# The rows of an expert block placed by a turned table of ranks

## The chip, the cores and the metric

The kernel runs on one core of a Trainium2 chip. The metric is the time of one execution on the device in microseconds (us); the median of several runs stands for the kernel. A core has TensorE (matmuls into PSUM), VectorE, ScalarE, GpSimd and SyncE (SP, which issues most transfers), and 16 DMA engines that carry all transfers between HBM and the on-chip memory (SBUF).

## The reference, cut to what matters

One inference step of one layer: a mixer (gated short convolution and sliding-window attention), a mixture of experts, and a gated per-layer embedding. 512 prompt tokens and 32 sample tokens pass through the same weights. The change touches only the mixture of experts:

```
logits = x @ w_router + b_router            # 544 tokens, 32 experts
top_v, top_i = top_k(logits, 4);  gate = softmax(top_v)
# for each expert e, on the tokens that chose it:
h = x @ w_up[e] + b_up[e]                   # 1024 -> 2048, glu and linear parts interleaved
act = min(glu, 7) * sigmoid(1.702 * min(glu, 7)) * (clip(lin, -7, 7) + 1)
y = act @ w_down[e] + b_down[e]             # 1024 -> 1024
out[token] = sum over its 4 experts of gate * y
```

All of it is in float32. 544 tokens with 4 experts each are 2176 pairs, 68 for an expert on average. In which order the tokens of one expert are computed doesn't matter to the result.

## The kernel before

After the mixer, the tokens' normalised rows (4 KB each) are written to a table m_rows in HBM. The router gives each token four experts. For each (token, expert) pair the kernel computes its rank among the tokens of that expert by matmuls with a triangular matrix (`rk0`), splits it into a lap (which block of the expert) and a `slot` below CAP = 96, and builds three things from it. The first two blocks have a short way of their own (`hot0`, `hot1`, lines 1511 and 1516), so that their gathers can start early. For all other blocks `slot_hots` (line 1591) makes a one-hot table `rank1` of slot against position: position p of a block is 1 where the table `iota` at p equals the pair's slot. Matmuls with it (`slot_rows`, line 2285) give, per block and position, the row number in m_rows (`rowi`), the row of the result table y_rows (`dsti`) and the gate (`gcol`). A position that no pair has gets a number beyond the table's end; the transfer of such a row is left out by its bounds check. `iota` holds 0, 1, 2, ..., so real rows are at positions 0 to n - 1 of a block with n tokens, and the padding is behind them.

The experts' loop runs over blocks of 96 positions (CAP = 32 * SETS); with these inputs there are 32, one for each expert. For block i:

- GpSimd gathers the rows: `rows_from` (line 692) is an indirect DMA from m_rows into `xg`, partition = position. VectorE transposes xg into xT (line 1650).
- TensorE multiplies: three bias matmuls (line 2259), then eight up chunks (line 2262) of 1 MB of w_up each; ScalarE and VectorE form the activation; VectorE transposes it (line 1659); four down chunks (line 2272) of 1 MB of w_down follow. The down matmuls of block i - 1 are done behind the up matmuls of block i.
- ScalarE and VectorE scale the result by the gate into `yrow` (lines 1014, 1639), and GpSimd scatters it to y_rows (`rows_to`, line 703), also an indirect DMA.

SP issues the weights (line 610). There are twelve chunk buffers `raw`, one block's worth: chunk l of the next block is issued when TensorE has used up chunk l of this one. Block STASH = 20 finds its first three chunks in three spare buffers (`ahead`) that were filled before the loop; one gate chunk for the layer's end (`gate_r`, line 620) is issued behind block 21.

The last block isn't scattered. Its result goes to the tokens by a matmul with `Sel` (line 1707), a one-hot table of token number (from `iota`) against the block's row numbers. At the end SP issues the last block's down chunks (line 632), three gate chunks (lines 634, 636, 638), and, once every scatter has landed, the rows of h and y_rows for each of five token tiles (lines 643 to 645). VectorE adds them (line 1731; for tiles 1 to 4 GpSimd sums pairs first, line 748); the embedding gate and the last norm follow. ScalarE rounds the gate chunks (line 1051) and VectorE splits them (line 1698).

`iota` is loaded by SP at line 556, between the last token tile's wait and its stores (lines 563 to 572), on the semaphore io_in, which line 1018 (ScalarE) and line 1508 (VectorE) wait for.

Of the kernel before, what the change touches and what calls it, by code (L numbers as in the profile page):

```python
# [13 lines left out]
F32 = mybir.dt.float32  # L14
# [7 lines left out]
P = 128  # L22
# [6 lines left out]
NT = 5  # L29
# [12 lines left out]
NEXP, TOPK = 32, 4  # L42
# [15 lines left out]
CAP = 32 * SETS  # L58
# [30 lines left out]
def build(nc, A, O):  # L89

    with ExitStack() as ctx:
        def sem(name):
            return ctx.enter_context(nc.semaphore(name))
# [5 lines left out]
        def at(name, shape, dt, off):  # L99
            n = int(np.prod(shape[1:])) * 4  # L100
            assert off + n <= 212800, (name, off + n)
            return nc.alloc_sbuf_tensor_at(name, shape, dt, offset=SB0 + off)
# [8 lines left out]
        R2 = R1 + 2 * KT * T * 4  # L111
# [89 lines left out]
        iota = at("iota", [P, P], F32, R2 + 4352)  # L201
        rank1 = at("rank1", [P, NT * TOPK, P], F32, R0)
# [3 lines left out]
        which = at("which", [P, NB], F32, R2 + 7168)  # L206
        plain = at("plain", [P, NB], F32, R2 + 7424)
        dstf = at("dstf", [P, NB], F32, R2 + 7680)
        bup = at("bup", [8, 512], F32R, R2 + 5120)
        bsel = at("bsel", [8, SETS, P], F32R, R2 + 35328)  # L210
        bself = at("bself", [8, SETS * P], F32, R1 + 16384)
        hot0 = at("hot0", [P, NT, P], F32, R2 + 7168)
        ent0 = at("ent0", [P, NT], F32, R2 + 9728)
        pad0 = at("pad0", [P, 1], F32, R2 + 9760)
        hot1 = at("hot1", [P, NT, P], F32, R2 + 9792)
# [180 lines left out]
        io_in = sem("io_in")  # L396
# [72 lines left out]
        def _(sp):  # L469
# [79 lines left out]
            for i in range(NT):  # L549
                if i == 1:  # L550
                    sp.wait_ge(tr_done, NT + 1)
                    sp.dma_start(raw[2][:], w_up[0, 2]).then_inc(landed[2], 16)
                if i == NT - 1:

                    sp.wait_ge(tiles_done, TB)
                    sp.dma_start(iota[:], A["c_iota"]).then_inc(io_in, 16)
                    sp.dma_start(bself[:], A["c_bsel"]).then_inc(io_in, 16)
                    for m in (4, 5):
                        sp.dma_start(raw[m][:], w_up[0, m]).then_inc(landed[m], 16)
                rows = slice(P * i, P * i + ROWS[i])  # L560
                sp.wait_ge(wo_ev, i + 1)
                if i < NT - 1:
                    sp.dma_start(h_dram[rows], hrow[:, i, :]).then_inc(h_out, 16)
                else:
                    for j in range(4):
                        sp.dma_start(h_dram[rows, QD * j:QD * j + QD], hrow[TS * j:TS * j + TS, i, 0:QD]).then_inc(h_out, 16)
                sp.wait_ge(m_done, i + 1)
                if i < NT - 1:
                    sp.dma_start(m_dram[rows], mrow[:, i % 2, :]).then_inc(rows_out[i % 2], 16)
                else:  # L570
                    for j in range(4):
                        sp.dma_start(m_dram[rows, QD * j:QD * j + QD], mrow[TS * j:TS * j + TS, i % 2, 0:QD]).then_inc(rows_out[0], 16)
# [179 lines left out]
        def _(act):  # L752
# [262 lines left out]
                                     scale=gcol[0:CAP, bass.ds(b, 1)]).then_inc(y_done, 1)  # L1015

            pp_copy(1)
            act.wait_ge(io_in, 32)
            nc.scalar.activation(bsel[:].rearrange("r b m -> r (b m)"), bself[:], ACT.Copy).then_inc(b_rnd, 1)
            pp_copy(2)  # L1020
            pp_copy(3)
# [142 lines left out]
        def _(dve):  # L1164
# [326 lines left out]
            for i in range(NT):  # L1491
# [10 lines left out]
                if i == 1:  # L1502
# [2 lines left out]
            b = R0S + ROUT * NT  # L1505

            nc.vector.tensor_tensor(ent0[:], mask[:, :, 0], tok1[:].rearrange("p (i k) -> p i k", k=TOPK)[:, :, 0], ALU.mult)
            dve.wait_ge(io_in, 32)
            dve.wait_ge(rk_mm, 1)
            place = ps[:, 0, 0:NT * NEXP].rearrange("p (i e) -> p i e", e=NEXP)  # L1510
            nc.vector.tensor_tensor(hot0[:], iota[:].unsqueeze(1).broadcast_to([P, NT, P]),
                                    place[:, :, 0].unsqueeze(2).broadcast_to([P, NT, P]), ALU.is_equal).then_inc(hot_done, 1)

            nc.vector.tensor_tensor(over[:], ps[:, 0, 200:201].broadcast_to([P, 2]), code[:, 1:3], ALU.is_gt).then_inc(r_step, 1)
            nc.vector.tensor_tensor(ent1[:], mask[:, :, 1], tok1[:].rearrange("p (i k) -> p i k", k=TOPK)[:, :, 0], ALU.mult)
            nc.vector.tensor_tensor(hot1[:], iota[:].unsqueeze(1).broadcast_to([P, NT, P]),
                                    place[:, :, 1].unsqueeze(2).broadcast_to([P, NT, P]), ALU.is_equal).then_inc(hot_done, 1)
            dve.wait_ge(r_step, b + 1)
            nc.vector.tensor_tensor(kov[:], over[:], code[:, 3:5], ALU.mult).then_inc(r_step, 1)
# [67 lines left out]
            def slot_hots(tiles):  # L1587

                for i in tiles:
                    mine = slice(TOPK * i, TOPK * i + TOPK)  # L1590
                    nc.vector.tensor_tensor(rank1[:, mine, :], iota[:].unsqueeze(1).broadcast_to([P, TOPK, P]),
                                            slot[:, mine].unsqueeze(2).broadcast_to([P, TOPK, P]), ALU.is_equal).then_inc(rank_hot, 1)

            def slot_table():
# [921 lines left out]
def constants():  # L2516
# [23 lines left out]
    for b in range(SETS):  # L2540
        bsel[[b, 4 + b], b, 0:CAP] = 1
        bsel[[SETS, 4 + SETS], b, CAP:] = 1
    out = {
        "c_fold": np.tile(np.eye(TS), (4, 1)),
        "c_ident": np.eye(P), "c_negd": negd, "c_biass": bias, "c_tok": tok, "c_code": code,
        "c_tri": p < np.arange(P)[None, :], "c_ones": np.ones((P, P)),
        "c_pad": TOPK * KROWS + 1 + p, "c_zero": np.zeros((T, D)), "c_bsel": bsel.reshape(8, SETS * P),
        "c_io16": np.broadcast_to(np.arange(MAXOVER), (P, MAXOVER)), "c_io32": np.broadcast_to(np.arange(NEXP), (P, NEXP)),
        "c_iota": np.broadcast_to(np.arange(P), (P, P)),
    }  # L2550
    return {k: np.ascontiguousarray(v.astype(f)) for k, v in out.items()}
```

## Time and profile before

| | |
|---|---|
| median of 3 runs | 1536.05 us (1535.56 to 1536.28) |
| the profiled execution | 1538.34 us, of which the span is 1536.50 us |
| TensorE busy | 1496.2 us, 97% of the span |
| VectorE, ScalarE, GpSimd busy | 48%, 16%, 7% |
| bytes moved | 492.04 MB, 320 GB/s over the span |
| the chain that ended last | TensorE 76%, DMA 10%, VectorE 5%, SP's queue 4% |

A block of the expert loop begins with its bias matmuls, so these mark the blocks in the trace: the first at 403 us, the last at 1395 us. Before them lie the mixer and the router, behind them the last sums and norms. The time to landing of a transfer counts from its issue on the queue until all of its parts, on all engines, have signalled. A chain of waits goes back from the last instruction to whatever released each step.

### The profile page before, as it was taken

Reading aid. Unit: us, or ns where it says so; the run is one execution under the profiler, and the core shown is the slowest. Engines: PE = TensorE matmul, PEld = TensorE weight load, DVE = VectorE, ACT = ScalarE, POOL = GpSimd, SP = SyncE. Lnnn points to the kernel's source line nnn. Section 1 sums busy time; section 2 is a strip of 40 time slices with the busy share of each in tenths; the row PEclk is TensorE's granted clock in tenths of the full one; section 3 lists DMA queues with packets and bytes.
Section 4 is the critical chain, followed back from the end, with each engine's and each line's share of the span. In section 5 each row is a group of like instructions: output and inputs, shape, how many; then the busy total and the mean of one; then the engine's idle time right before and its main releaser. Section 6 shows DMA issues by size and latency. Waiting matters only on the chain.

```text
span 1536.5 us, 38278 instructions
## 1 busy us (share of the span) xinstructions
PE 1496.2 (97%) x16304; PEld 854.4 (56%) x16304; DVE 731.9 (48%) x1619; ACT 243.2 (16%) x443; POOL 103.1 (7%) x136
## 2 busy tenths in 40 slices
PE   8999999999999999999999999999999999999697
PEld 7999999998543334433344333443334433334396
DVE  5457333353545434554345543455434554336584
ACT  5433323232200000000000000000000000001244
POOL 1000000000000000000000000000000000000050
PEclk9999999999999999999999999999999999999899
DMA  7411922352999999999999999999999999999841
GB/s 262 157 56 55 306 93 83 114 212 106 374 407 403 408 407 410 407 398 404 408 410 407 400 402 407 402 388 398 407 411 400 404 396 402 401 404 383 315 159 46
DMA packets 83474, 492.04 MB, mean 320 GB/s; under 512 B 13950, under 2 KB 19174, under 8 KB 30052
## 3 DMA queue, kind: packets, MB, share of 16 engines
q1 hardware_dynamic: 76260, 473.51, 78.4%
q0 software_dynamic: 7056, 17.56, 3.3%
q8 instruction: 49, 0.80, 0.2%
q14 instruction: 13, 0.11, 0.0%
q10 hardware_dynamic: 96, 0.07, 0.0%
HBM read 478.45 MB, written 29.79 MB: 331 GB/s over the span
## 4 chain that ended last, share of the span: by engine, by line
PE 76%; DMA 10%; DVE 5%; SPq 4%; ACT 2%; issue 1%; POOL 0%; DVEq 0%; ACTq 0%
PE ps L2262 36%; PE ps L2272 18%; PE ps L1913 9%; DMA raw<-w_up 6%; PE ps L2103 3%; SPq L610 2%; DMA raw<-w_ple_chunks 2%; PE ps L1853 1%; PE ps L2259 1%; PE ps L1854 1%; PE ps L1855 1%; DVE hq L1731 1%; PE ps L1977 1%; ACT S L836 1%; SPq L598 1%
## 5 line engine op out<-in xcount | busy, mean ns | idle before, releaser
L2262 PE MATMUL ps<-raw,xT 128*32 128x512 f32 x6072 | 660.7, 593 | 2.9 <-DMA raw<-w_up 2.7
L2262 PEld LDWEIGHTS ps<-raw,xT 128*32 128x32 f32 x6072 | 192.2, 110 | 454.4 <-issue 423.7
L2272 PE MATMUL ps<-raw,acT 128*32 128x256 f32 x6144 | 338.1, 379 | 3.1 <-DMA raw<-w_down_rows 3.1
L2272 PEld LDWEIGHTS ps<-raw,acT 128*32 128x32 f32 x6144 | 199.4, 110 | 149.0 <-issue 18.3
L1626 DVE TENSOR_SCALAR gl<-ps 128x256 f32<-128x256 f32 x96 | 34.8, 418 | 451.0 <-ACT gl L1009 451.0
L1659 DVE STREAM_TRANSPOSE acT<-arow 32x192 f32<-32x192 f32 x512 | 189.3, 370 | 7.4
L1650 DVE STREAM_TRANSPOSE xT<-xg 32x256 f32<-32x256 f32 x372 | 161.9, 435 | 13.8 <-DMA xg<-m_rows,ius 8.2
L1009 ACT ACTIVATE gl<-ps 128x256 f32<-128x256 f32 x96 | 29.9, 384 | 662.3 <-PE ps L2262 662.3
L1913 PE MATMUL ps<-aTh,wh 128*128 128x272 f32 x512 | 107.3, 291 | 1.5 <-DVE qTl L1317 1.0
L1913 PE MATMUL ps<-aTh,wl 128*128 128x272 f32 x512 | 106.0, 288 | 0.0
L1913 PE MATMUL ps<-aTl,wh 128*128 128x272 f32 x512 | 105.6, 288 | 0.0
L1168 DVE TENSOR_TENSOR wl<-raw,wh 128x2048 fp32r<-128x2048 f32 x21 | 48.1, 2290 | 80.4 <-ACT wh L756 80.4
L1913 PEld LDWEIGHTS ps<-aTh,wh 128*128 128x128 f32 x512 | 80.2, 188 | 2.8 <-DVE wl L1168 1.3
L1639 DVE TENSOR_SCALAR yrow<-ps,gside 32x256 f32<-32x256 f32 x93 | 45.6, 490 | 75.3 <-PE ps L2272 74.4
L1913 PEld LDWEIGHTS ps<-aTl,wh 128*128 128x128 f32 x512 | 80.5, 188 | 0.0
L1913 PEld LDWEIGHTS ps<-aTh,wl 128*128 128x128 f32 x512 | 80.0, 189 | 0.0
L1014 ACT ACTIVATE yrow<-ps,gcol 96x768 f32<-96x768 f32 x31 | 27.8, 897 | 294.6 <-PE ps L2272 294.6
L692 POOL DMA_INDIRECT xg<-m_rows,iug x29 | 28.7, 991 | 387.7 <-DVE iug L1531 361.2
L697 POOL COPY iug<-rowi 128x1 uint32 x28 | 9.3, 331 | 574.0 <-DVE xT L1650 574.0
L756 ACT ACTIVATE wh<-raw 128x2048 fp32r<-128x2048 f32 x21 | 40.1, 1911 | 20.7 <-PE ps L1913 11.4
L703 POOL DMA_INDIRECT y_rows<-yrow,ius x30 | 28.4, 947 | 160.2 <-issue 160.2
L1853 PE MATMUL ps<-gate_h,nTh 128*128 128x256 f32 x128 | 38.2, 299 | 0.2 <-DVE nTl L1783 0.2
(385 smaller groups left out, 1310.3 us busy)
## 6 DMA issues: line engine op xcount, KB each, us to landing
raw<-w_up SPq DMA_DIRECT2D x253, 1024.0 KB, 21.9
raw<-w_down_rows SPq DMA_DIRECT2D x128, 1024.0 KB, 23.9
raw<-w_mix SPq DMA_DIRECT2D x25, 1024.0 KB, 4.9
y_rows<-c_zero SPq DMA_DIRECT2D x4, 2176.0 KB, 21.6
yk<-y_rows SPq DMA_DIRECT2D x8, 1024.0 KB, 11.3
raw<-w_ple_chunks SPq DMA_DIRECT2D x4, 1024.0 KB, 27.6
ahead<-w_up SPq DMA_DIRECT2D x3, 1024.0 KB, 15.2
xin<-x_prompt SPq DMA_DIRECT2D x4, 512.0 KB, 6.3
```

The source lines that it names most:

```text
L610: sp.dma_start(raw[l][:], src).then_inc(landed[l], 16)
L756: nc.scalar.activation(wh[slot][:], raw[s][:], ACT.Copy).then_inc(rounded, 1)
L1168: nc.vector.tensor_tensor(wl[slot][:], raw[s][:], wh[slot][:].bitcast(F32), ALU.subtract)\
L1626: nc.vector.tensor_scalar(gl[:, 1, b, :], src, LIMIT + 1.0, 1.0 - LIMIT, ALU.min, ALU.max).then_inc(lin_done, 1)
L1639: ins = nc.vector.tensor_scalar(yrow[32 * g:32 * g + 32, SETS * LB:], ps[CAP:P, 3 + g, 0:LB], gside[CAP:P, g, bass.ds(b, 1)], None, ALU.mult)
L1650: ins = nc.vector.transpose(dst[32 * r:32 * r + 32, :, 32 * g:32 * g + 32], xg[32 * g:32 * g + 32, :].rearrange("p (k n) -> p k n", n=P)[: ...
L1659: ins = nc.vector.transpose(dst[32 * r:32 * r + 32, :, 32 * g:32 * g + 32], arow[32 * g:32 * g + 32, :].rearrange("p (k n) -> p k n", n=P) ...
L1853: mmul(out, ah, bh, start=first, stop=False)
L1913: ins = mmul(out[:, 512 * b:512 * b + HALF], w, a[:, k, HALF * b:HALF * b + HALF], start=(k == 0 and a is aTh and w is lh), stop=(k == KT ...
L2103: ins = mmul(out[:, 512 * b:512 * b + HALF], w, y[:, CT * r + k, HALF * b:HALF * b + HALF], start=(k == 0 and w is lh and y is yTh), stop= ...
L2262: ins = mmul(ps[32 * j:32 * j + 32, b, :], xT[:, k, 32 * g:32 * g + 32], w[:, 512 * q:512 * q + 512], start=False, stop=(k == UPC - 1))
L2272: ins = mmul(ps[32 * j:32 * j + 32, bank + b, 0:LB], a, raw[slot][:, D * (k % 2) + LB * q:D * (k % 2) + LB * q + LB], start=(k == 0), stop ...
```

## The change

A second table `turn` is made beside `iota` and takes its place in the three compares that turn ranks into positions (`hot0`, `hot1`, `rank1`). Position p of the first 96 holds rank p // 6 + 16 * (p % 6), so rank 0 is at position 0, rank 1 at 6, rank 2 at 12, and so on to rank 15 at 90; rank 16 is at position 1. The table is loaded by one more DMA, and both waits on io_in go from 32 to 48. `Sel` still uses `iota`.

```diff
+        turn = at("turn", [P, P], F32, R2 + 13312)
...
                     sp.wait_ge(tiles_done, TB)
                     sp.dma_start(iota[:], A["c_iota"]).then_inc(io_in, 16)
+                    sp.dma_start(turn[:], A["c_turn"]).then_inc(io_in, 16)
                     sp.dma_start(bself[:], A["c_bsel"]).then_inc(io_in, 16)
...
-            act.wait_ge(io_in, 32)
+            act.wait_ge(io_in, 48)
...
-            dve.wait_ge(io_in, 32)
+            dve.wait_ge(io_in, 48)
...
-            nc.vector.tensor_tensor(hot0[:], iota[:].unsqueeze(1).broadcast_to([P, NT, P]),
+            nc.vector.tensor_tensor(hot0[:], turn[:].unsqueeze(1).broadcast_to([P, NT, P]),
...
-            nc.vector.tensor_tensor(hot1[:], iota[:].unsqueeze(1).broadcast_to([P, NT, P]),
+            nc.vector.tensor_tensor(hot1[:], turn[:].unsqueeze(1).broadcast_to([P, NT, P]),
...
-                    nc.vector.tensor_tensor(rank1[:, mine, :], iota[:].unsqueeze(1).broadcast_to([P, TOPK, P]),
+                    nc.vector.tensor_tensor(rank1[:, mine, :], turn[:].unsqueeze(1).broadcast_to([P, TOPK, P]),
...
+    each = CAP // 16
+    turn = np.where(np.arange(P) < CAP, np.arange(P) // each + 16 * (np.arange(P) % each), np.arange(P))
```

## Rows read from the trace of the kernel before

**Rows 1.** Page and stretches: busy us of each engine (x instructions), PEclk, DMA share, GB/s.
```profile
PE 1496.2 (97%) x16304; PEld 854.4 (56%) x16304; DVE 731.9 (48%) x1619; ACT 243.2 (16%) x443; POOL 103.1 (7%) x136
...
402.00:1187.00 785.00, 784.25 (x9338) 313.80 (x9339) 357.81 (x902) 46.11 (x99) 58.37 (x92) 1.00 1.01 404
1187.00:1394.00 207.00, 204.17 (x2506) 81.40 (x2502) 96.14 (x240) 11.93 (x27) 14.67 (x24) 1.00 1.01 402
```

**Rows 2.** Chain in order of time, one block: start us, us, what.
```profile
526.86 20.74 PE ps L2262 x192
547.59 10.36 PE ps L2272 x192
557.95 0.89 PE ps L2259 x3
```

**Rows 3.** Two starts from the timeline, and waits of 1190 to 1450: us, times, longest.
```profile
1197.62 0.96 PE L2259 MATMUL ps<-bup,bsel 8*128 8x512 f32 x3
...
1394.76 0.96 PE L2259 MATMUL ps<-bup,bsel 8*128 8x512 f32 x3
...
PEld ps L2262 <- DMA raw<-w_up: 28.2, 39, 1.4
```

**Rows 4.** Issues to landing (last number), windows from 528, 944, 1040, 1080, 1205.
```profile
raw<-w_up SPq DMA_DIRECT2D x8, 1024.0 KB, 14.3
...
raw<-w_up SPq DMA_DIRECT2D x8, 1024.0 KB, 26.8
...
raw<-w_up SPq DMA_DIRECT2D x8, 1024.0 KB, 20.7
...
raw<-w_up SPq DMA_DIRECT2D x8, 1024.0 KB, 25.2
...
raw<-w_up SPq DMA_DIRECT2D x8, 1024.0 KB, 28.2
```

**Rows 5.** Queue 0 (packets, MB, share of 16 engines' span), and gathers' landing.
```profile
q0 software_dynamic: 7056, 17.56, 3.3%
...
xg<-m_rows,iug POOLq DMA_INDIRECT x29, 8.7
```

**Rows 6.** Timeline of the end: start us, us, engine, line, what, idle before.
```profile
1419.19 2.02 SPq L638 DMA_DIRECT2D raw<-w_ple_chunks  x1
...
1439.07 0.33 SPq L643 DMA_DIRECT2D hq<-h_rows  x1
...
1439.24 2.80 PE L2272 MATMUL ps<-raw,acT 128*32 128x256 f32 x48 [0.52 <-DMA raw<-w_down_rows]
...
1441.60 1.91 ACT L1051 ACTIVATE gate_h<-raw 128x2048 fp32r<-128x2048 f32 x1 [11.49 <-DMA raw<-w_ple_chunks]
...
1448.24 1.50 DVE L1736 TENSOR_SCALAR yn<-ps,gate 32x256 f32<-32x256 f32 x3
...
1451.16 5.06 DVE L1731 TENSOR_TENSOR hq<-hq,yk 128x1024 f32<-128x1024 f32 x4
...
1460.25 6.79 POOL L748 TENSOR_TENSOR yk<-yk 128x1024 f32<-128x1024 f32 x2 [27.76 <-DMA yk<-y_rows]
...
DMA to landing us min/median/max: 27.6/27.6/27.6
```

**Rows 7.** Timeline around the load of iota: SP's queue, and VectorE's first compare.
```profile
379.34 0.33 SPq L556 DMA_DIRECT2D iota<-c_iota  x1
...
380.94 2.11 SPq L566 DMA_DIRECT2D h_rows<-hrow  x4
384.78 2.71 SPq L572 DMA_DIRECT2D m_rows<-mrow  x4
...
388.49 0.82 DVE L1511 TENSOR_TENSOR hot<-iota,ps 128x640 f32<-128x640 f32 x1 [1.63 <-PE ps L2234]
```

**Rows 8.** GB/s in 0.8 us slices from 528 us; GpSimd's gather before it.
```profile
GB/s 415 282 323 323 348 369 389 451 410 410 430 399 425 433 417 430 420 440 430 410 420 420 420 440 410 430 420 410 420 440 420 410 440 410 410 420 430 440 410 420
...
524.10 0.98 POOL L692 DMA_INDIRECT xg<-m_rows,iug  x1 [0.93 <-issue]
```

More of the change, by code:

```diff
@@ L2548, in constants @@
         "c_io16": np.broadcast_to(np.arange(MAXOVER), (P, MAXOVER)), "c_io32": np.broadcast_to(np.arange(NEXP), (P, NEXP)),
-        "c_iota": np.broadcast_to(np.arange(P), (P, P)),
+        "c_iota": np.broadcast_to(np.arange(P), (P, P)), "c_turn": np.broadcast_to(turn, (P, P)),
     }
```

## The prediction, made before the changed kernel was run

> **What bounds the kernel now.** I read the page first: TensorE is busy for 97% of the span [rows 1]. Such a number invites the answer that a change to transfers can bring nothing, so the second view was the chain in order of time. In the expert loop it holds TensorE alone: one block is 0.89 us of bias matmuls, 20.74 us of up matmuls and 10.36 us of down matmuls, 31.99 us together [rows 2], and this pattern repeats with nothing between for some 23 blocks. The third view was the same loop near its end. Six blocks between the bias matmuls at 1197.62 and 1394.76 take 197.14 us, and 6 x 31.99 is 191.94: 5.20 us are lost, and the waits name weight chunks (w_up) that had not landed [rows 3]. So the loop begins bound by TensorE and ends bound by transfers.
>
> Why it turns is seen in the time from the issue of a weight chunk to its landing, window by window: 14.3 us at 528, 26.8 us at 944, 20.7 us after the stash (three chunks that block 20 finds loaded already), then 28.2 us, where it stops growing, because TensorE now waits [rows 4]. From 528 to 944 are 13 blocks: 12.5 us / 13 = 0.96 us more delay with each block. A chunk's buffer comes back about one block after its issue was allowed, so about 29 us is all the delay that is hidden. The transfers are not short of this on average: one block needs 12.58 MB of weights, 2 x 68 rows of 4 KB (0.56 MB) and 0.02 MB of biases, 13.16 MB in 31.99 us or 411 GB/s, and they moved 404 GB/s [rows 1], 1.7% or 0.55 us per block less. The landing time grows faster than that mean lag (0.96 us), and a chunk has landed only when the slowest of 16 engines has its part. That points at unequal engines.
>
> **The inequality.** Queue 0 carries only the row gathers and scatters: 7056 packets and 17.56 MB [rows 5]. 32 gathers and 31 scatters with 96 + 16 packets each are 7056 packets; 17.56 MB are 4287 rows of 4 KB, which is 2 x 2176 real rows less the 65 of the last block, which isn't scattered. The other slots are padding, with an index out of bounds, and move nothing. A block thus has 68 real rows in 96 slots, and before the change they are slots 0 to 67. If an engine serves six neighbouring slots (96 / 16), engines 0 to 10 move 6 rows, engine 11 moves 2 and engines 12 to 15 none, in every gather and scatter. The price of a row packet: 3.3% of 16 x 1536.5 us is 811 us, over 4287 rows 0.189 us [rows 5].
>
> **The change, part by part.** (1) The turned table puts rank r on slot 6 (r mod 16) + r / 16, so every engine gets 4 or 5 of 68 rows. A full engine goes from 12 row packets per block to 8.5 on average: 3.5 x 0.189 = 0.66 us less; the low engines get 5 + 5 at times: 2.5 x 0.189 = 0.47 us less. The delay of the slowest then grows 0.96 - 0.47 to 0.66 = 0.3 to 0.5 us per block; I take 0.4. (2) Carried through: 14.3 us at block 4, + 16 x 0.4 = 20.7 at block 20. The stash and the extra chunk behind it (gate_r) together take off about 5 us: from 26.8 at 944, 4.25 blocks of 0.96 would be 30.9 at 1080, and 25.2 are seen [rows 4]. That leaves 15.7 us, and ten more blocks make it 20, well under 29. All 5.20 us of stalls in the loop go. (3) The last block. It starts at 1394.76 and its last matmul ends at 1439.24 + 2.80 = 1442.04 [rows 6], 47.28 us. Without stalls it is 0.89 + 20.74 + 10.36 + 0.85 (the transposes between) + 10.36 = 43.20: 4.08 us go. The end of TensorE's expert work moves from 1442.04 to 1389.56 + 43.20 = 1432.8. (4) Behind it, before: ScalarE sits until 1441.60 for a gate chunk, rounds two chunks, and so takes the last block's result late; VectorE splits both chunks and starts it at 1448.24, and the first h add comes at 1451.16 [rows 6]. With a delay of 20 us both gate chunks land by 1430 or so, the rounding and splitting lie beside the last matmuls, and TensorE's side would allow that add at 1432.8, plus 2.9 of work as from 1448.24 to 1451.16, plus some 0.5 to start: 1436.2. (5) What is late next are the rows of h and y. Their loads are issued when the last scatter has landed (1439.07 [rows 6]); that scatter follows the down matmuls of the block before, which move up by 5.20 + 1.7, so it lands at about 1432.2. On the engines they stand behind the last gate chunk, issued at 1419.19 and landing 27.6 us later, at 1446.8; GpSimd's pair sums of tile 1, for which 5.2 MB must be in, start at 1460.25 [rows 6], 13.4 us after it. With the change that chunk is issued at about 1389.56 + 24.2 = 1413.8 and lands 20 us later, at 1433.8: tile 1 is in at 1447.2, 13.0 us earlier. If the delay grows by only 0.3 us a block, the scatter sets it, 1432.2 + 13.4, 14.6 us earlier. I take 13.0, the middle value of the growth. The tail after it keeps its length. Of this 9.3 us are TensorE's stalls, and 3.7 the wait behind them.
>
> (6) The added load of the table: 64 KB and one more instruction on the SP queue, ahead of bself, of raw 4 and 5 and of the last h and m rows. It takes 0.33 us of issue like iota's [rows 7], some 0.4 with the gap behind it. The h rows go out 0.4 us later; behind them SP waits until 384.78 for m, and h would end at 383.4 instead of 383.05, 1.4 us ahead of that: nothing behind moves. VectorE and ScalarE wait for 48 instead of 32 on the same semaphore; VectorE needs the table at 388.49, 8.8 us after its issue at 379.7, and then TensorE ends its wait, not a transfer [rows 7]. Queued behind that wait are the first hot table and with it the first gather. Cost 0, up to 0.4 us if the cover fails. (7) The compares with turn in place of iota have the same shape: 0. Sel keeps iota, and matches the row numbers of whatever slot holds them: 0.
>
> **Sum.** -5.2 - 4.1 - 3.7 = -13.0 us, plus 0. The profiled execution took 1538.34 us with a span of 1536.50; the median of three is 1536.05. The span becomes 1523.5, and by the same step of -13.0 the median becomes 1523.0 us, 0.8% less.
>
> **A page against the trace.** While a gather runs the core moves 282 to 369 GB/s for some 4 us instead of 410 to 440 [rows 8] (the gather is issued at 524.10, and its rows follow within its landing time of 8.7 us). The Trainium skill (SBUF — State Buffer, Door 1: The DMA port swizzle) has partitions 0 to 63 on only eight of the sixteen ports. By that rule the real rows before crowd half the ports, and spread over 96 partitions they would not; the dip would shrink, and the delay would grow by less than 0.4 us a block. No row shows ports apart, so the sum leaves it out.
>
> **Rivals.** (A) The sum of the engines is at its limit, not the loaded ones. For it: 404 GB/s in the long stretch and 402 in the end [rows 1], never the 411 needed. Then evenness helps little: (411 - 402) / 411 x 32 = 0.7 us per block on every engine, the delay reaches 14.3 + 11.2 - 5 + 7 = 27.5 us at the end, the loop's stalls go nearly all, but the last gate chunk lands at 1413.8 + 27.6 = 1441.4, 5.4 us earlier than now: 1530.6 us. Against it: windows of 0.8 us at 440 and 451 are common [rows 8]. Chance 0.2. (B) Slots are dealt another way (slot mod 16): then rows are already even and stay so, and nothing changes: 1536. Against it: the landing time outgrows the mean lag by 0.4 us per block. Chance 0.04. (C) Slower: one of the five engines without rows is slow in itself, and no view shows them apart, since a chunk's landing is the slowest engine's. It now gets 8.5 row packets, 1.6 us per block. The present slowest needs 31.99 + 0.96 = 32.95 us per block; if such an engine needs over 31.35 us for its weights alone, it becomes a worse brake than today's. At 31.55 the transfers take 0.2 us per block more, 6 us over 30 blocks: 1542 us. Against it: its weights alone, from the slowest loaded engine, are 32.95 - 12 x 0.189 = 30.7 us. Chance 0.04. The Trainium skill (DMA: Bandwidth & Descriptors, Latency and other measured facts) calls engines 7 and 15 usually slower; engine 15 would be such a one.
>
> **Chances and range.** Forecast 0.72, its own range 1520.5 (the scatter sets it, and a little of the tail goes too) to 1528 (0.6 us per block, 25 us of delay); A 0.2, B 0.04, C 0.04. To hold 8 in 10 the range reaches into A: 1520.5 to 1531. A measurement of this kernel can tell about 0.2%, 3 us, from no change. Faster by more than that: the forecast and A, 0.92 less a little for A turning out worse: 0.91; within: 0.05; slower: 0.04.
>
> **What would show it.** Right: blocks of 31.99 us up to the last one; landing medians that grow by 0.3 to 0.5 us per block and stay under 25; gather landings a little under 8.7 us [rows 5]; ScalarE's wait for the gate chunk gone; SP issues never stretched to 2 us. Wrong in (1): landing times growing as fast as now. Wrong in (5): the first h add is early but tile 1's pair sums still start after 1455. Wrong in (6): VectorE's wait at the first hot table ended by the table's load. What would sink the number: a limit on the sum (A) or a slow idle engine (C).

## The result, and the profile after

The changed kernel takes 1520.11 us (median of 4 runs, 1518.77 to 1521.53) where the kernel before takes 1536.15 (4 runs, 1535.56 to 1536.28): ratio 0.9894, 95% interval 0.9882 to 0.9905. That is 16.0 us less. 13.0 us were forecast, and the time lies 0.4 us under the range's low end.

The profiled execution has a span of 1516.92 us against 1536.48, 19.6 us less. 3.5 us of this are no effect of the change: the profiled run of before lay 2.3 us above its median [the table under "Time and profile before"], that of after 1.3 us below. The page of the changed kernel, its rows for engines, queue 0 and the chain:

```profile
PE 1491.5 (98%) x16304; PEld 855.8 (56%) x16304; DVE 730.9 (48%) x1619; ACT 243.0 (16%) x443; POOL 99.0 (7%) x136
...
q0 software_dynamic: 7056, 17.56, 3.4%
...
PE 90%; DVE 5%; ACT 2%; DMA 2%; issue 1%; SPq 1%; DVEq 0%; ACTq 0%
```

Queue 0 carries the same packets and bytes as in [rows 5]; only where they go has changed. In the chain the transfers' share was 10% and is now 2%. The two long stretches of the expert loop (columns as in [rows 1]), changed kernel:

```profile
402.00:1187.00 785.00, 783.78 (x9356) 313.88 (x9352) 356.33 (x900) 45.01 (x100) 57.69 (x92) 1.00 1.01 408
1187.00:1389.00 202.00, 202.00 (x2501) 83.01 (x2496) 96.24 (x241) 11.69 (x25) 14.66 (x24) 1.00 1.01 412
```

In the second stretch TensorE is busy in every microsecond, where it lacked 2.83 us in [rows 1], and the last number says what feeds it: 412 GB/s, the 411 that a block of 31.99 us needs, against 402. The landing times of w_up, changed kernel, windows from 528, 944, 1040, 1080 and 1205 us as in [rows 4] (the last number):

```profile
raw<-w_up SPq DMA_DIRECT2D x8, 1024.0 KB, 10.9
...
raw<-w_up SPq DMA_DIRECT2D x8, 1024.0 KB, 13.8
...
raw<-w_up SPq DMA_DIRECT2D x8, 1024.0 KB, 8.4
...
raw<-w_up SPq DMA_DIRECT2D x9, 1024.0 KB, 11.1
...
raw<-w_up SPq DMA_DIRECT2D x9, 1024.0 KB, 10.8
```

From 528 to 944 the delay grows by 2.9 us in 13 blocks, 0.22 us per block against 0.96. It never comes near the 29 us that are hidden. The end of the changed kernel in the timeline (start us, us, engine, line, what, in brackets the idle time before it):

```profile
1388.07 0.96 PE L2261 MATMUL ps<-bup,bsel 8*128 8x512 f32 x3
...
1412.41 0.33 SPq L640 DMA_DIRECT2D raw<-w_ple_chunks  x1
...
1420.79 10.57 PE L2274 MATMUL ps<-raw,acT 128*32 128x256 f32 x192
1421.59 3.71 ACT L1053 ACTIVATE gate_h<-raw 128x2048 fp32r<-128x2048 f32 x2
1423.15 0.93 POOL L705 DMA_INDIRECT y_rows<-yrow,ius  x1 [0.94 <-issue]
1426.40 0.33 SPq L645 DMA_DIRECT2D hq<-h_rows  x1
...
1431.42 1.50 DVE L1738 TENSOR_SCALAR yn<-ps,gate 32x256 f32<-32x256 f32 x3 [3.40 <-PE ps L2274]
...
1434.35 5.06 DVE L1733 TENSOR_TENSOR hq<-hq,yk 128x1024 f32<-128x1024 f32 x4
...
1442.16 4.70 POOL L750 TENSOR_TENSOR yk<-yk 128x1024 f32<-128x1024 f32 x2 [18.08 <-DMA yk<-y_rows]
```

The last block's down matmuls run in one piece of 192, where [rows 6] shows the last 48 of them waiting for w_down. ScalarE rounds both gate chunks beside them; the wait of 11.49 us of [rows 6] is gone. VectorE takes the last result 0.06 us after TensorE is done (1431.36), and its idle time is ended by TensorE, no longer by a transfer.

The difference of the two profiled executions, cut at the marks of [rows 3], [rows 6] and the fence above:

| stretch | before | after | difference |
|---|---|---|---|
| start to the first block's bias matmuls | 402.78 | 400.73 | -2.05 |
| from there to the last block's | 991.98 | 987.34 | -4.6 |
| last block, to TensorE's last expert matmul | 47.28 | 43.29 | -4.0 |
| from there to the first h add | 9.12 | 2.99 | -6.1 |
| h add to the end of the span | 85.32 | 82.57 | -2.75 |

SP's issues are no longer stretched. The same work on its queue, first in the kernel before and then in the changed one (timeline):

```profile
1403.41 10.42 SPq L632 DMA_DIRECT2D raw<-w_down_rows  x4
```

```profile
1391.95 8.04 SPq L634 DMA_DIRECT2D raw<-w_down_rows  x4
...
1402.10 0.34 SPq L636 DMA_DIRECT2D raw<-w_ple_chunks  x1
1404.67 0.34 SPq L638 DMA_DIRECT2D raw<-w_ple_chunks  x1
```

The three gate chunks took SP 2.25, 2.18 and 2.02 us to issue before (the last in [rows 6]), and take 0.34, 0.34 and 0.33 now.

### The profile page after: what moved, and what is told of

The parts are those of the page before. It is cut to its first block, busy times and chain, and to the rows that moved or that the text cites. A ratio compares the mean times of both kernels' runs of the same rounds, so it can differ in the third digit from the quotient of the medians.

```text
span 1516.9 us, 38279 instructions
## 1 busy us (share of the span) xinstructions
PE 1491.5 (98%) x16304; PEld 855.8 (56%) x16304; DVE 730.9 (48%) x1619; ACT 243.0 (16%) x443; POOL 99.0 (7%) x136
## 3 DMA queue, kind: packets, MB, share of 16 engines
q0 software_dynamic: 7056, 17.56, 3.4%
## 4 chain that ended last, share of the span: by engine, by line
PE 90%; DVE 5%; ACT 2%; DMA 2%; issue 1%; SPq 1%; DVEq 0%; ACTq 0%
PE ps L2264 43%; PE ps L2274 22%; PE ps L1915 10%; PE ps L2105 3%; PE ps L2261 2%; PE ps L1855 2%; PE ps L1856 2%; PE ps L1857 2%; DVE hq L1733 1%; DMA raw<-w_up 1%; PE ps L1979 1%; ACT S L838 1%; DVE S L1226 1%; PE ps L2122 0%; PE ps L2420 0%
## 6 DMA issues: line engine op xcount, KB each, us to landing
raw<-w_up SPq DMA_DIRECT2D x253, 1024.0 KB, 11.6
```

## The experiments

The theory on trial: the engine with the most row packets sets how fast the landing time grows, and that growth sets both the stalls in the loop and the wait behind it. The kernels differ in which engine gets how many rows, or in which transfers carry rows at all. Times of a kernel are compared with the runs of before on the same chip, which came out at 1536.5 to 1537.8 us. "Growth" is always the landing time of w_up in the window from 944 us less that from 528 us, over 13 blocks.

**1. The table loaded, but not used (load_only).** The changed kernel, with iota back in the three compares (hot0 is shown, hot1 and rank1 go the same way).

```diff
-            nc.vector.tensor_tensor(hot0[:], turn[:].unsqueeze(1).broadcast_to([P, NT, P]),
+            nc.vector.tensor_tensor(hot0[:], iota[:].unsqueeze(1).broadcast_to([P, NT, P]),
```

> The table is loaded, but the three compares still use iota, so the rows lie as before. Theory (the whole gain is in where the rows lie, the load costs next to nothing): 1536 to 1537 us, since in the profile of the change the first block's last up chunk lands 0.7 us later after its issue than before. If the gain came from anything else in the change, it would be near 1520.

Measured: 1536.65 us (10 runs), ratio 1.0004 (0.9994 to 1.0015). So the whole gain is in the placing, and the extra load costs nothing that shows. Its stretch of the timeline:

```profile
378.06 0.33 SPq L557 DMA_DIRECT2D iota<-c_iota  x1
378.43 0.43 SPq L558 DMA_DIRECT2D turn<-c_turn  x1
...
387.20 0.82 DVE L1513 TENSOR_TENSOR hot<-iota,ps 128x640 f32<-128x640 f32 x1 [1.63 <-PE ps L2236]
...
401.50 0.93 PE L2261 MATMUL ps<-bup,bsel 8*128 8x512 f32 x3
```

From iota's issue to the first bias matmul are 23.44 us; in the kernel before they are 402.78 - 379.34 = 23.44 too [rows 7]. VectorE's wait is ended by TensorE in both.

**2. As many rows on the fullest engines, but other engines (high_end).** Rank r at position 95 - r: engines 5 to 15 carry the rows, eleven of them in full.

```diff
-    turn = np.where(np.arange(P) < CAP, np.arange(P) // each + 16 * (np.arange(P) % each), np.arange(P))
+    turn = np.where(np.arange(P) < CAP, CAP - 1 - np.arange(P), np.arange(P))
```

> Rank r is placed at position 95 - r: the real rows lie at positions 28 to 95. Ten or eleven engines still get six rows, now engines 5 to 15, and 34 of 68 rows lie on partitions 0 to 63 instead of 64. Engines alone (the fullest engine's 12 row packets set the delay): landing time grows by about 0.96 us per block and reaches 28 us as before, 1535 to 1537 us. Half of the partitions alone (rows crowded on partitions 0 to 63 slow the gather): growth near 0.2 us per block, as with the turned table, and 1519 to 1522 us. Both: growth of 0.5 to 0.8, 1522 to 1534 us. A slow engine among 12 to 15, idle in gathers and scatters before: growth over 1.1 us per block and more than 1538 us.

Measured: 1530.21 us (4 runs), ratio 0.9957 (0.9941 to 0.9974). The landing times from 528 and 944 us, and the end in the timeline:

```profile
raw<-w_up SPq DMA_DIRECT2D x8, 1024.0 KB, 13.7
...
raw<-w_up SPq DMA_DIRECT2D x8, 1024.0 KB, 22.9
...
1388.55 0.96 PE L2261 MATMUL ps<-bup,bsel 8*128 8x512 f32 x3
...
1433.62 1.91 ACT L1053 ACTIVATE gate_h<-raw 128x2048 fp32r<-128x2048 f32 x1 [11.44 <-DMA raw<-w_ple_chunks]
```

The growth is 0.71 us per block, between before (0.96) and after (0.22). The delay passes 27 us only in the last blocks, so the loop has no stall, while ScalarE's wait for the gate chunk is as long as before (11.44 against 11.49 us) and the way from the last expert matmul to the h add is 9.19 us. Most of the growth is there with the same 12 packets on other engines, so it is no property of engines 0 to 10; a quarter of it is not explained by the count. One number of the expectation is a slip: positions 28 to 63 lie on partitions 0 to 63, which is 36 of 68 rows and not 34. The turned table has 48 there and before 64.

**3. Ten row packets on the fullest engines (fives).** Five of each engine's six positions are used first, so with 68 rows engines 0 to 12 carry 5 + 5.

```diff
+    q, g = np.arange(P) % each, np.arange(P) // each
+    turn = np.where(np.arange(P) < CAP, np.where(q < 5, 5 * g + q, 80 + g), np.arange(P))
```

> Engine e gets ranks 5e to 5e + 4 and rank 80 + e: 68 rows put five rows on engines 0 to 12, so the fullest have 10 row packets per block where before has 12 and the turned table 8.5 on average. Growth of the landing time linear in these packets (0.96 at 12, 0.22 at 8.5): 0.54 us per block, a delay of about 21 us at the end, no stall in the loop (31.99 us per block to the end). My step (5) with 21 us of delay: the row loads at the end, not TensorE, set the first sums, some 2 to 4 us later than with the turned table: 1522 to 1525 us. If the size of the delay doesn't matter as long as it stays under 29 us: 1520 to 1521 us. If the sum of the engines were the limit, 1520 to 1521 too, with the growth of the turned table.

Measured: 1524.04 us (4 runs), ratio 0.9923 (0.9907 to 0.994). Landing times from 528 and 944 us, and the end:

```profile
raw<-w_up SPq DMA_DIRECT2D x8, 1024.0 KB, 12.2
...
raw<-w_up SPq DMA_DIRECT2D x8, 1024.0 KB, 17.9
...
1430.55 0.33 SPq L645 DMA_DIRECT2D hq<-h_rows  x1
...
1437.87 5.07 DVE L1733 TENSOR_TENSOR hq<-hq,yk 128x1024 f32<-128x1024 f32 x4
```

Growth 0.44 us per block, between after and before. To set it against the packets, these have to be counted on the fullest engine, and 8.5 is not that count: it is the mean of all sixteen. The kept traces have each gather's row packets of 4 KB, 54 to 85 of them. The turned table gives rank r to engine r mod 16, so engine 0 always has the rounded-up share: 4 rows in nine blocks, 5 in twenty, 6 in three, with gather and scatter 9.6 packets per block. In fives the fullest engine has 10.2, in before 12. So 12, 10.2 and 9.6 packets give 0.96, 0.44 and 0.22, which is 0.29 and 0.31 us less for each packet less. This is the dose curve of the theory, and it is steeper than the forecast's 0.189. TensorE's part is that of the changed kernel to 0.1 us, yet the h add starts 6.43 us after the last expert matmul instead of 2.99. A delay of some 20 us (landing time from 1340 us) costs the loop nothing and the tail 3.4 us: the gate chunks land 25.1 us after their issue, ScalarE waits 5.60 and 1.38 us for them, and VectorE splits the second one ahead of the last result.

**4. The changed kernel without the stash (turn_nostash).** Block 20 loads all of its chunks in the loop.

```diff
-        lead = [1, 1, 1] + [0] * 9
+        lead = [0] * 12
...
-            for l in range(3):
-                sp.dma_start(ahead[l][:], w_up[STASH, l]).then_inc(ahead_in, 16)
...
-                stash = isinstance(i, int) and i == STASH
+                stash = False
```

> The changed kernel without the three chunks of block 20 that are loaded ahead; they are loaded in their place, so 7.5 us of transfers come back into the loop. Theory (the turned table leaves a delay of 11 us of the 29 that are hidden): delay 16 to 19 us in the last blocks, every block 31.99 us, 1519 to 1523 us. If transfers were still near their limit: stalls in the last blocks and more than 1525 us.

Measured: 1526.21 us (4 runs), ratio 0.9922 (0.99 to 0.9945), so by the ratios 2 to 4 us and by the medians 6 us slower than the changed kernel. Its own runs go from 1520.87 to 1527.6 and the intervals overlap (0.9882 to 0.9905 there), so the times alone don't settle it; the waits below do show a later tail. The landing time, 11.0 us from 944, comes to 15.8 us from 1205 and 18.0 from 1340 (12.8 in the changed kernel). From the fourth on, every block of the loop still takes 31.99 us. What is lost lies behind it:

```profile
1438.59 5.07 DVE L1729 TENSOR_TENSOR hq<-hq,yk 128x1024 f32<-128x1024 f32 x4 [1.76 <-DMA yk<-y_rows]
...
1448.04 6.80 POOL L746 TENSOR_TENSOR yk<-yk 128x1024 f32<-128x1024 f32 x2 [21.55 <-DMA yk<-y_rows]
```

Here the rows of tile 0 set the h add, as step (5) had it, and tile 1's sums begin 9.4 us after it instead of 7.8. I had taken any delay under 29 us for free. That holds for the loop alone.

**5. Rows at both ends (outer).** Positions 0 to 33 and 62 to 95: engines 0 to 4 and 11 to 15 are full.

```diff
+    c = np.arange(P)
+    turn = np.where(c < 34, c, np.where((c >= 62) & (c < CAP), c - 28, np.where(c < CAP, c + 34, c)))
```

> 68 real rows at positions 0 to 33 and 62 to 95: engines 0 to 4 and 11 to 15 get six rows, 36 rows lie on partitions 0 to 63. high_end had 34 on partitions 0 to 63 and its delay grew by 0.71 us per block instead of 0.96, but it also left engines 0 to 3 without rows. If crowded halves made the difference: growth about 0.7 us per block, 1529 to 1532 us. If it was that the lowest engines had no rows (they also carry the 4-partition bias loads, or are slower): growth 0.9 to 1.0 as before, 1535 to 1538 us.

Measured: 1533.28 us (10 runs), ratio 0.9977 (0.9964 to 0.9989). The landing time from 944 us, and from 1205:

```profile
raw<-w_up SPq DMA_DIRECT2D x8, 1024.0 KB, 22.7
...
raw<-w_up SPq DMA_DIRECT2D x9, 1024.0 KB, 26.0
```

Growth (22.7 - 12.5) / 13 = 0.78 us per block. Only the last two blocks of the loop are long, 32.66 and 32.87 us. The time lies between the two expectations, so this run decides neither for the halves of the partitions nor for the lowest engines. It has 36 of 68 rows on partitions 0 to 63, as high_end has, and the same 12 packets; the 0.07 us between their growths has neither cause.

**6. More bytes, the same fullest engines (pads_scatter).** The kernel before, with the padding rows of each scatter written to an unused row of the result table: 28 more packets of 4 KB in a block, 0.11 MB, and every engine has 6 rows in the scatter.

```diff
-        "c_pad": TOPK * KROWS + 1 + p,
+        "c_pad": T + 1 + p,
```

> The kernel before, but the padding's index lies in an unused part of y_rows, so that every scatter writes 96 rows: engines 0 to 10 still six, engines 12 to 15 now six instead of none, 0.11 MB more per block (2.8 MB or so in all). What the padding writes is not read. Fullest engine: growth stays 0.96 us per block, 1536 to 1538 us. Sum of the engines as the limit: 28 rows at 410 GB/s are 0.28 us more per block, 8 us over the loop, 1542 to 1546 us. A slow engine among 12 to 15: slower still.

Measured: 1536.07 us (10 runs), ratio 1.0 (0.999 to 1.001). From 944 us, and the start of the last block:

```profile
raw<-w_up SPq DMA_DIRECT2D x8, 1024.0 KB, 27.2
...
1392.29 0.97 PE L2259 MATMUL ps<-bup,bsel 8*128 8x512 f32 x3
```

Growth (27.2 - 14.5) / 13 = 0.98. If the sum of the engines were at its limit (rival A), 0.9% more bytes would cost 0.28 us in each of 30 blocks, up to 8 us. They cost nothing. The added work, on engines that are not the fullest, was free.

**7. The changed kernel again (after_again)**, on the chip of runs 5 and 6.

> The changed kernel once more, beside the others on one chip: 1519 to 1522 us if the first result holds, with a last gate chunk that lands in 12 to 13 us and a last scatter that lands 3 to 4 us after its issue.

Measured: 1520.56 us (4 runs), ratio 0.9907 (0.9891 to 0.9924). The first result holds beside another set of runs. Growth (12.9 - 10.8) / 13 = 0.16 us per block; its way from the last expert matmul to the h add is 2.99 us again.

**8. iota's load out of the way (iota_late).** The changed kernel, with iota, which only Sel needs now, loaded in the loop behind the first gate chunk on a semaphore of its own that VectorE waits for ahead of Sel.

```diff
-                    sp.dma_start(iota[:], A["c_iota"]).then_inc(io_in, 16)
+            sp.dma_start(iota[:], A["c_iota"]).then_inc(late_in, 16)
...
-            act.wait_ge(io_in, 48)
+            act.wait_ge(io_in, 32)
...
+            dve.wait_ge(late_in, 16)
```

> The changed kernel with iota, which only Sel still needs, loaded inside the loop behind the gate chunk; before the loop one table is loaded as in the kernel before. If the added load costs the first block 0.6 us (its last up chunk lands that much later): 0.5 us faster than the changed kernel, first block 26.5 instead of 27.1 us. If that was chance: no difference.

Measured: 1519.88 us (4 runs), ratio 0.99 (0.9884 to 0.9917). It is the lowest median of all kernels here, but it cannot be told from the changed kernel's. From the table's issue at 377.56 to the first bias matmul at 401.81 are 24.25 us, no less than the 23.54 of the changed kernel. Its first block takes 26.26 us where the changed kernel has 27.12 and 27.03 in its two profiles. But high_end and outer, which load both tables ahead of it, have 26.26 too and load_only 26.47, so the 0.6 us don't follow the load.

**9 and 10. One kind of row transfer taken away (no_gather, no_scatter).** The kernel before, with the indices of the gathers of all blocks but the first two, or of all those scatters, out of bounds, so that their rows are left out; the kernels compute on stale rows, or lack those blocks' part of the result. The fullest engine has 6 row packets per block in both.

```diff
-                nc.vector.tensor_copy(rowi[:, 0:NB], padi[:]).then_inc(row_step, 1)
+                nc.vector.tensor_scalar(rowi[:, 0:NB], padi[:], 4096.0, None, ALU.add).then_inc(row_step, 1)
```

```diff
-                nc.vector.tensor_copy(dsti[:], dstf[:]).then_inc(row_step, 2)
+                nc.vector.tensor_scalar(dsti[:], dstf[:], 8192.0, None, ALU.add).then_inc(row_step, 2)
```

> The kernel before without its gathers from block 2 on: their indices all lie out of bounds, so no row is read, and the blocks compute with stale rows. The scatters stay, six rows on each full engine. In the kernel before the core moves about 320 instead of 420 GB/s for some 4 us beside each gather; the scatter shows no such dip. If the gather costs its six packets (6 x 0.189 = 1.1 us on a full engine) and slows all weights besides (4 us x 100 / 420 = 0.95 us): the transfers gain 2.1 us per block, the delay falls from 12 us to its floor of about 6 us within eight blocks and stays there, 1516 to 1521 us. If the gather costs only its packets: growth 0.96 - 1.13 = -0.2 us per block, the delay is still about 9 to 10 us at 944 us.

> The kernel before without its scatters (all their indices out of bounds, no row is written); the gathers stay. If a scatter costs only its packets (1.0 to 1.1 us on a full engine) and slows nothing else: growth 0.96 - 1.05 = -0.1 us per block, a delay that stays at 10 to 12 us through the loop, no stalls, 1517 to 1521 us. If scatter and gather cost the same in all: the same landing times as without the gathers.

Measured: without gathers 1521.97 us (4 runs), ratio 0.9897 (0.9876 to 0.9918); without scatters 1521.9 us (4 runs), ratio 0.9901 (0.9884 to 0.9917). Landing times from 528 and 944 us, first without gathers, then without scatters:

```profile
raw<-w_up SPq DMA_DIRECT2D x8, 1024.0 KB, 7.7
...
raw<-w_up SPq DMA_DIRECT2D x8, 1024.0 KB, 6.9
```

```profile
raw<-w_up SPq DMA_DIRECT2D x8, 1024.0 KB, 12.0
...
raw<-w_up SPq DMA_DIRECT2D x8, 1024.0 KB, 12.1
```

Neither grows. The fullest engine has the same number of rows in both, yet with the gathers left in a chunk lands after 12 us and without them after 7. A gather delays the weights by more than the packets that a scatter has too. The kept trace of before shows it packet by packet (from 490 to 990 us): a weight packet of 8 KB takes 315 ns on average while no rows move, 314 beside a scatter and 421 beside a gather. A row packet itself takes 160 ns in a scatter and 207 in a gather. In the time of the kernel both give the same: the delay is below what either the loop or the tail feels.

**All kernels beside each other.** Row packets per block on the fullest engine (mean of the blocks), growth as above, the landing time of the last three gate chunks (window from 1390 us), the last block, the way from TensorE's last expert matmul to the first h add, and the median time.

| kernel | packets | growth | gate chunks land | last block | to the h add | median |
|---|---|---|---|---|---|---|
| no_gather | 6 | -0.06 | 9.7 | 43.29 | 2.99 | 1521.97 |
| no_scatter | 6 | 0.01 | 14.6 | 43.29 | 2.99 | 1521.90 |
| after | 9.6 | 0.22 | 16.1 | 43.29 | 2.99 | 1520.11 |
| turn_nostash | 9.6 | 0.20 | 21.9 | 43.29 | 4.82 | 1526.21 |
| fives | 10.2 | 0.44 | 25.1 | 43.29 | 6.43 | 1524.04 |
| high_end | 12 | 0.71 | 27.5 | 45.50 | 9.19 | 1530.21 |
| outer | 12 | 0.78 | 28.3 | 47.70 | 9.19 | 1533.28 |
| load_only | 12 | 0.95 | 27.9 | 47.41 | 9.14 | 1536.65 |
| pads_scatter | 12 | 0.98 | 27.7 | 48.04 | 9.14 | 1536.07 |

Read down, it shows two prices of one cause. The loop and the last block pay only when the delay comes near 27 us. The way to the h add pays sooner: nothing at 16 us, 1.8 at 22, 3.4 at 25, 6.2 at 27.5.

**The sixteen parts of a chunk.** The traces don't number the engines, but each weight chunk signals sixteen times, once for each engine's part. Medians over the chunks that land from 944 to 1040 us, as the lead of a part over the last one: in before five parts are 19.3 to 20.0 us early, the next 14.7 and 10.3, the other nine 0 to 6.4. With six neighbouring positions per engine, engines 11 to 15 have 0 to 5 row packets per block there, engine 10 has 8.9 and engine 9 has 10.6. In fives the first five parts are 13.1, 12.9, 12.9, 11.6 and 9.1 us early, and engines 15 to 11 have 1.2, 2.9, 5.1, 7.6 and 8.7 packets. In the changed kernel (after_again) no part leads by more than 6.8 us and the last three land within 0.3 us of each other; engines 0 to 3 are its fullest. In no_gather all sixteen land within 1.0 us. So the engines are unequal, and as unequal as that dealing makes them. A chunk is late by its last part alone.

## Why the prediction was wrong in its size, and right in its direction

**(1) The growth per block: the term that was mis-sized.** 0.96 less 0.47 to 0.66 was to leave 0.3 to 0.5, and I took 0.4; 0.22 was measured, and 0.16 to 0.25 in the other three kernels with the turned table. Two errors stand in the term, and they pull in opposite directions. The count: the fullest engine goes from 12 packets to 9.6, 2.4 less and not 3.5, and the low engines get 5 + 5 in most blocks (twenty experts of 32 have 65 to 80 rows) and not just at times. With the forecast's price this would save 0.45 us and leave 0.51. The price: a packet less on the fullest engine took 0.31 us off the growth (0.74 over 2.4 packets), and 0.29 in fives, where the forecast had 0.189. So the step that failed is what the turned table saves on the fullest engine per block: 0.47 to 0.66 us forecast, 0.74 measured, from too many packets saved at too low a price. That the two errors cancel in part is luck. How far the price is the packets' alone is taken up under "The page against the trace". A smaller slip beside it: the last block has 68 rows and not 65. The trace has 4284 row packets of 4 KB, and 4287 came from the rounded 17.56 MB.

Why the price was too low can be read in part. 0.189 us is a packet's own time, between the 160 ns of a scatter and the 207 of a gather. It leaves out that a gather slows the weights beside it, from 315 to 421 ns per packet (396 in the changed kernel, 414 in fives). An estimate from these: in before a gather's rows take 3.60 us to pass, of which a full engine spends 6 x 0.207 = 1.24 on rows; in the other 2.36 it moves weights a quarter more slowly and loses 0.59; with 6 x 0.160 = 0.96 for the scatter, that is 2.80 us per block. The same sum gives 2.16 for the changed kernel (4.8 rows, 2.93 us) and 2.37 for fives (5.1 rows, 3.11 us). So 0.63 of the 0.74 us are covered, and 0.43 of the 0.52. The rest, about 0.1 us, is open.

The slowing is seen in the rate of the core too. Slices of 0.8 us from 528 us, changed kernel, fives and high_end (before in [rows 8]):

```profile
GB/s 297 307 369 430 410 430 420 407 433 420 389 410 446 430 420 440 410 410 440 420 430 399 440 410 420 430 420 430 420 420 410 430 420 430 420 430 410 430 410 292
```

```profile
GB/s 282 292 312 358 440 389 430 410 430 430 379 430 415 440 410 420 440 430 420 410 420 410 440 420 430 430 399 420 420 440 430 420 420 399 420 430 440 420 405 312
```

```profile
GB/s 297 317 343 287 343 440 379 399 389 451 425 394 425 420 440 430 430 430 389 451 410 430 451 389 440 410 420 451 399 451 379 451 410 410 461 389 451 389 440 343
```

At the start of each row, the slices under 370 GB/s are five in before, five with high_end, four with fives and three in the changed kernel. This gather has 68 rows: the fullest engines have 6, 6, 5 and 5 of them, but thirteen engines have 5 in fives and four in the changed kernel. Over 16 windows of 32 us from 528 us on, what the slices lack to 415 GB/s adds up to 0.65 MB per window for before, 0.66 for high_end, 0.60 for fives and 0.575 for the changed kernel. But after_again has 0.62, and pads_scatter, with the gathers of before, 0.57. So this sum is too coarse to price the dip.

**(2) The delay at the end: 20 us forecast, 12.8 seen** (landing time from 1340 us). Two slips add up. The growth, by (1). And the start: I carried the 14.3 us that before has at block 4, though four changed blocks lie ahead of it; the changed kernel has 10.9 there. With the measured growth, 10.9 + 16 x 0.22 = 14.4, less 5 for the stash, plus ten blocks of 0.22 gives 11.6. That all of the loop's stalls go was right: -5.20 forecast, and from the fourth block on every one takes 31.98 or 31.99 us to the end. The loop as a whole gained 4.6, since its first block took 0.6 us more (27.12 against 26.54 us). It is not the extra load: load_only has 26.47.

**(3) The last block: right.** 43.20 us forecast, 43.29 seen.

**(4) TensorE's side of the h add: right in kind.** 3.4 us after the last expert matmul were allowed for, 2.99 seen, and only TensorE ends VectorE's wait.

**(5) What is late next: wrong, as a consequence of (1) and (2).** I let the rows of h and y set the end, at -3.7 us behind TensorE. They are not late. The last scatter was to land at 1432.2. It is issued at 1423.15, and SP, which waits for its landing, issues the h load at 1426.40: 3.3 us, where before it took 1439.07 - 1431.56 = 7.5 us. I had carried the 7.5 us over unchanged. The delay of the chunks alone doesn't set this time: in the loop, from 528 us, a scatter lands after 7.5 us in before and 7.4 in the changed kernel, and at the end after 7.3 us in fives and 6.8 in turn_nostash. That fewer chunks stand ahead of it at the end is the likely reason and isn't shown. So TensorE sets the h add, and -6.1 us are had behind it instead of -3.7. fives is nearly the case that I had forecast: its delay at the end is 20 us, it gains 9.12 - 6.43 = 2.7 us behind TensorE where the forecast had 3.7, and its median is 12.5 us under that of before on its chip, where the forecast had 13.0. Its tile 1 sums start at 1446.43, where the forecast had 1447.2. So the path of (5) came out at that delay. Step (4) did not: its h add comes at 1437.87 instead of 1436.2, because there the gate chunks were still waited for.

With the forecast's own steps and the measured dose, -5.2 - 4.1 - 6.1 = -15.4 us, 0.6 us from the medians' -16.0. The profiled stretches give 4.6 + 4.0 + 6.1 = 14.7 us for the same three. Of the other 4.8 us, 2.05 lie before the first block, where before was merely late in that execution (the first block starts between 399.2 and 404.0 us in the twelve profiles, whatever the placing), and 2.75 behind the h add. About 1.7 of these are TensorE's clock. Granted clock in the third column from the right, first before, then after_again:

```profile
1508.50:1512.50 4.00, 4.00 (x23) 4.00 (x22) 2.54 (x4) 1.92 (x3) 0.00 (x0) 0.57 0.00 0
```

```profile
1488.00:1492.50 4.50, 3.96 (x27) 3.94 (x28) 2.35 (x4) 3.04 (x5) 0.00 (x0) 0.62 0.05 18
```

A mean of 0.57 over 4 us is 3.4 us at the lower level, 1.2 GHz, while TensorE works, which costs half of that. Such a stretch shows in before and in after_again, in high_end, turn_nostash, no_gather and no_scatter, and in the last 40 us of neither the first profile of the changed kernel nor the other five, so it belongs to an execution and not to the change. The remaining 1 us behind the h add has no cause that I can name.

**(6) The extra load costs nothing: right**, 23.44 us in both [rows 7], and ratio 1.0004. **(7)** right.

**The page against the trace.** The forecast left the port rule out of the sum. What the runs say of it is mixed. high_end and outer (both 36 of 68 real rows on partitions 0 to 63) grow by 0.71 and 0.78 us per block, before (64) by 0.96, all three with 12 packets on the fullest engines. But the dip of high_end is no shorter than that of before: a gather's rows take 3.59 us to pass there and 3.60 in before, and a weight packet beside them 418 and 421 ns. The Trainium skill (SBUF — State Buffer, Door 1: The DMA port swizzle) would have fewer rows on the lower half of the partitions relieve the ports there; the growth agrees with it, the dip does not. Halves alone are refuted: the turned table (48 rows there) and fives (54) have more rows on the lower half than high_end and outer, and grow less, by 0.22 and 0.44. Beside the engines, up to 0.25 us per block could be the halves' part, for 28 rows. In proportion the turned table's 16 rows less would have 0.14 of its 0.74 us and fives' 10 less 0.09 of 0.52, and a packet would cost 0.25 and 0.24 us, still more than 0.189. But if what sets high_end and outer apart from before is something else, and the turned table and fives share it in full, a packet costs only 0.15 to 0.23 us (0.71 or 0.78 less 0.44 over 1.8 packets, less 0.22 over 2.4). It stays open, and with it whether the 0.1 us left in (1) is that. Which rows lie on which engine can't be changed apart from which partitions they lie on, in these kernels.

**The rivals.** A (a limit on the sum) is refuted twice: 412 GB/s over 202 us of the changed kernel, and 0.11 MB more per block for nothing. (Against it I had called windows at 440 and 451 common; [rows 8] has 451 once.) B (slots dealt in another way) is refuted by load_only against the changed kernel: with B, the placing would be worth nothing. The five early parts of a chunk in before speak for six neighbouring positions per engine. C (a slow engine among the idle ones) found no support: in high_end engines 11 to 15 carry 12 packets each and the growth is less than before. The Trainium skill (DMA: Bandwidth & Descriptors, Latency and other measured facts) calls engines 7 and 15 usually slower; no run here shows it.

## What to carry to other kernels

When a large transfer has to land on all engines, its delay follows the fullest engine, not the mean: if landing times grow from block to block while the mean rate lags by less, count the packets of every small indirect transfer per engine, on the fullest one and not as a mean, and spread the real rows (here 68 of 96) over all of them. A packet's own time is not its whole price where it slows its neighbours. A delay that a loop hides behind its buffers is not free: everything issued near the loop's end inherits it, and here the tail began to pay between 16 and 22 us, long before the loop did at 27. And when a change alters a growth, carry it from the first block, not from the first window that was read.

## What the runs showed of the hardware

- An indirect DMA over 96 rows is cut into runs of six neighbouring rows per engine: turning the order of rows, with the same packets and bytes, is worth 16 us, five rows used of every six give the dose in between, and the leads of a chunk's sixteen parts fit this dealing (five parts 19 to 20 us early in before, where five engines have few or no rows).
- A row that is left out still is a packet, of 4 bytes: the trace of before has 4284 row packets of 4 KB and 2772 of 4 bytes on queue 0. 63 x 96 positions less 4284 are 1764 of padding, and 63 x 16 signals make up the rest.
- A gather from HBM slows other transfers, and in the kernel before a scatter with the same rows doesn't: a weight packet of 8 KB takes 421 ns beside a gather, 314 beside a scatter and 315 otherwise. Chunks land after 12 us with the gathers alone left and after 7 us with the scatters alone left.
- The core moved 412 GB/s over 202 us, more than the 402 to 404 that looked like a ceiling in the kernel before.
- SP takes longer to issue when the engines are far behind: 2.0 to 2.8 us for each of the first two gate chunks of 1 MB in the kernels whose gate chunks land after 27.5 us or more, 0.34 us in the others, fives with 25.1 us among them.
- The last scatter lands 3.3 us after its issue in the changed kernel and 7.3 to 7.7 us after it where the gate chunks take 25 us or more.
